# RWKV groups 1 to 3 of a hybrid decoder trunk: whole value projection ahead of the triangular matrices, output projection between and behind them

## The chip, the cores and the metric

The kernel runs on one core of one Trainium2 chip. The metric is the device time of one execution in microseconds (us), where less is better; the time of a kernel is the median of several runs. A change of 0.5% is about what a measurement of this kernel can tell from no change.

## What is computed

One RWKV-7 time-mixing layer with its SwiGLU, then one layer of dilated sliding-window attention with its SwiGLU, on 256 tokens of 1024 columns in float32. The change lies in the time mixing:

```python
def rwkv7_time_mix(x, ...):
    h = rms_norm(x, norm_g)
    dx = jnp.pad(h, ((0, 0), (1, 0), (0, 0)))[:, :-1] - h
    xr, xw, xk, xv, xa, xg = (h + dx * mu[i] for i in range(6))
    r = xr @ w_r
    ...
    k = xk @ w_k
    v = xv @ w_v
    ...
    o = wkv7_scan(rh, decay, kh, vh, -kk, kk * ah)
    ...
    o = (o - mean) * lax.rsqrt(var + LNX_EPS)
    o = o.reshape(Bn, Sn, Dn) * lnx_g.astype(f32) + lnx_b.astype(f32)
    bonus = jnp.sum(rh * kh * r_k.astype(f32), axis=-1, keepdims=True) * vh
    y = (o + bonus.reshape(Bn, Sn, Dn)) * g.astype(f32)
    return y.astype(x.dtype) @ w_o, v_first
```

The scan is computed in chunks: products of decayed keys give triangular matrices over 128 tokens, and (1 - triangle) is inverted block by block.

## The kernel before, in words

Time mixing runs in four **groups** of four heads (256 columns); `group(it)` exists once for each engine (PE L631, ACT L1170, DVE L1676), and each engine works through its own list in the order of the code, held to the others by semaphores alone. A group projects r, k and v, builds the matrices for two chunks (c = 0, 1) of 128 tokens, inverts them, applies them, and normalises the output. From group 1 on weights and inputs are split in a high and a low float32r part, and a product is three matmuls (hi by hi, lo by hi, hi by lo; `PASSES`). Group 0 uses float32 and has no work left over (`behind=False`).

The output projection of group it - 1 (`product_o(it)`, L598) runs inside group it. It multiplies the gated output y (`y_hi`, `y_lo`) by `ow_hi` and the low part of w_o: two tiles of 128 tokens by two halves of 512 columns, six matmuls of 512 columns each. The result goes to the PSUM banks of `WO_BANKS` (L243), and DVE adds it to the residual stream x (`add_output`, L1670, one call for each of four quarters; it counts `dve_xadd`).

**PE, group 1 to 3.** Second rank of the decays; r; v quarter 0 (12 matmuls of 256 columns); `turn_norms`; v quarter 1; `product_o` tile 0; wait for `dve_scaled` (all inputs of the matrices); matrices of c = 0 (eight matmuls); `product_o` tile 1; matrices of c = 1; then the inversion levels l = 1 to 5 (L751). Each level is X products for heads 0 to 3 and 4 to 7, U products for both, and a filler, `values_fill(l)` (L710): v quarter 2 between the two X products of level 1 (l = 0), v quarter 3 and transposes of the keys after level 1, then bonus and gate in levels 2 and 3, the turned values in level 4, a product with `Vn` in level 5. After the levels come transposes (L782), the last block of the inversion, `next_keys(v)`, which is a quarter of the next group's k projection (in group 3, matmuls that only keep the clock), and the state.

**DVE, group 1 to 3.** Norms of the last group's output, scans, gates; then `gate_output` (L1659: two `stt`, a sync, and y + bonus), the copy of the next gains to `pl`, `decayed_keys`, the low part of y after ACT has made `y_hi`, `receptances`, `unit_keys`, and the last product, which counts `dve_scaled`. Then `add_output` 0 and 1; the masked copies of the c = 0 matrices, a reduction and a block transpose (T, counted by `dve_T`); `add_output` 2 and 3; the same for c = 1; and the levels. `low_key_weights(0)` and `(1)` (L1706) follow levels 1 and 2: the low part of the next group's k weights, one half each.

**ACT, group 3** (L1170 on): after the matrices it waits for `pe_v`, issues the load of a norm gain, copies `vT`, copies the turned keys, and then

```python
act.wait_ge(s_gu[0], 32)
A(wsp[:, 1, 0, 0:2048], raw[0][:, 0:2048], ACT.Copy).then_inc(S("act_gu_hi"), 1)
act.wait_ge(s_dn[0], 16)
A(wsp[:, 1, 0, 2048:3072], raw[0][:, 2048:3072], ACT.Copy).then_inc(S("act_dn_hi"), 1)
...
act.wait_ge(S("pe_g"), it + 1)
...
A(gT, bank[5], ACT.Copy).then_inc(S("act_g"), 1)
act.wait_ge(S("pe_tv"), it + 1)
A(Vn.rearrange("p c n i -> p (c n i)"), bank[6], ACT.Copy).then_inc(S("act_vn"), 1)
```

The first two copies are the high parts of the first gate/up and down weights of the feed-forward part. The four copies of the inverted blocks to `Us` (L1263) follow. In groups 1 and 2 the copies of the next group's `rw_hi` and of `ow_hi` (which waits for this group's w_o weights, `s_wm[3]`, and for all four quarters of `product_o`) stand where group 3 has the feed-forward ones.

**SP** issues the loads in one list: for each group k, r, w_o (`load_out`, L392) after `pe_wo` has counted all quarters of `product_o`, v after `pe_v`, and the second-rank weights. At the end of the list for time mixing stand

```python
sp.wait_ge(S("pe_wo"), NGRP * 4 - 4)
load_out(NGRP - 1)
```

and right behind, with no wait of their own that is still open there, the feed-forward loads: gate/up (two of 512 KB) and down (512 KB) for slot 0, the same for slot 1.

Of the kernel before, what the change touches and what calls it, by code (L numbers as in the profile page):

```python
# [16 lines left out]
ALU = mybir.AluOpType  # L17
# [71 lines left out]
def program(nc, ins, out):  # L89
    ctx = ExitStack()  # L90
    with ctx:
# [150 lines left out]
        HALVES = (slice(0, KT * T // 2), slice(KT * T // 2, KT * T))  # L242
        WO_BANKS, WO_LAST = (0, 1, 7, 0), (0, 1, 5, 7)  # L243
        EARLY = 2
# [248 lines left out]
        def _(pe):  # L493
# [104 lines left out]
            def product_o(it, tiles=range(RT), done=0, halves_=range(2)):  # L598
# [8 lines left out]
                for r in tiles:  # L607
                    for j in halves_:
                        if r == 1 and j == 1 and it < NGRP:
                            pe.wait_ge(S("dve_xadd"), it * 4 - 3)  # L610
                        o = bank[(WO_BANKS if it < NGRP else WO_LAST)[2 * r + j]]
# [19 lines left out]
            def group(it, behind=True, ahead=True):  # L631


                def next_keys(v):
                    if ahead:
                        if v == 0:
                            pe.wait_ge(S("dve_x_lo"), 2)
                            pe.wait_ge(S("dve_mix_lo"), it * 6 + 2)
                        project_parts(7, 1, kw_hi, (xk_hi, xk_lo), "pe_k", [v])
                    else:  # L640
                        keep_clock((4, 4, 4, 3)[v], 7)
# [45 lines left out]
                if behind:  # L687
                    turn_norms()
                    values([early - 1])
                    pe.wait_ge(S("act_sa"), it + 1)  # L690
                    product_o(it, [0])
                pe.wait_ge(S("dve_scaled"), it + 1)
                for c in range(2):
                    if c == 1:
                        if behind:
                            product_o(it, [1])
                        else:
                            values([early - 1])
# [11 lines left out]
                def values_fill(l):  # L710

                    if l == 0:
                        values(range(early, 3))
                    elif l == 1:
                        values(range(max(early, 3), 4))
                        for j, src in enumerate((kP, bP)):
# [34 lines left out]
                for l in range(1, LEVELS - 1):  # L751
                    corner = l == LEVELS - 2
                    for q in range(2):
                        pe.wait_ge(S("dve_T"), it * 10 + 2 * l + q - 1)
                        if l == 1 and q == 0 and behind:
                            pe.wait_ge(S("dve_xadd"), it * 4)
                        for u in range(4 * q, 4 * q + 4):
# [736 lines left out]
        def _(dve):  # L1494
# [143 lines left out]
            def norm_output(it, c, meanwhile=None, squaring=None):  # L1638
# [18 lines left out]
                tt(on[:, c, :, :].rearrange("p n (h i) -> p (n h) i", h=2), occ, wide_[1], ALU.mult).then_inc(S("dve_on"), 1)  # L1657

            def gate_output(it, c=None):  # L1659

# [15 lines left out]
            def group(it, behind=True, ahead=True):  # L1676
# [97 lines left out]
                if behind:  # L1774
                    gate_output(it)
                    q.mark(dve.tensor_copy(pl[:, :, :], par[:, two, lg:lg + 2]))
                    decayed_keys()
                    dve.wait_ge(S("act_y_hi"), it)
                    low_part(y_lo[:, :, :], yT[:, :, :], y_hi[:, :, :], "dve_y_lo")
                    receptances()  # L1780
# [19 lines left out]
                if behind:  # L1800
                    add_output(it, [0, 1])
                def turn_blocks(h):
# [5 lines left out]
                for c in range(2):  # L1808
# [10 lines left out]
                    if behind and c == 0:  # L1819
                        add_output(it, [2, 3])  # L1820
                    if not behind and c == 0:
# [3 lines left out]
                for l in range(1, LEVELS - 1):  # L1825
# [9 lines left out]
                    for h in range(2):  # L1835
# [7 lines left out]
                        else:  # L1843
                            for o, i in PAIRS:
                                m = dve.tensor_copy(Us[o, us, i], new[o])
                            m.then_inc(S("dve_U"), 1)
                    if ahead and l in (1, 2):
                        low_key_weights(l - 1)
                    if l == 3:
# [5 lines left out]
                for n in range(2):  # L1855
                    cut = slice(n * T, (n + 1) * T)
                    m = stt(bv[:, cut], bv[:, cut], pl[:, n, 1:2], gT[:, cut], ALU.add, ALU.mult)
                q.mark(m)
                for h in range(2):
                    dve.wait_ge(S("pe_X"), it * 12 + 11 + h)  # L1860
# [313 lines left out]
```

## Time and profile before

| What | Value |
|---|---|
| median of 3 runs | 937.66 us (937.49 to 942.2) |
| the profiled execution: time | 938.9 us |
| its span | 936.6 us |
| granted TensorE clock, mean of the span | 0.996 |
| PE / DVE / ACT / POOL busy | 919.4 / 685.3 / 501.9 / 100.5 us |
| time mixing, groups 1 to 3 | about 88 to 266 us of the span |

All times in the rows below count from the start of the span. L495 is the line of the matmul helper `mm`, L1496 and L1499 are `tt` and `stt`, L1102 is ACT's helper: the tile names tell the operations apart. `wide` is banks 3 to 6 of PSUM, `bank` the others.

### The profile page before, as it was taken

The numbers are of one execution on the slowest core, as the hardware profiler recorded it, in microseconds if no ns is written. First come the engines' busy times: TensorE is split into PE (matmuls) and PEld (weight loads), VectorE is DVE, ScalarE is ACT, GpSimd is POOL, SyncE is SP. The second block draws the span as 40 slices with busy tenths as digits, with TensorE's granted clock in tenths as the row PEclk, the third lists the DMA queues.
The fourth block names the chain that finished last, engine by engine and source line by source line (L and its number), as shares of the span: only waits on it lengthen the run. The fifth ranks groups of instructions, "written<-read, shape, count | busy, mean of one in ns | idle before, by whom it ended". The sixth has DMA issues, their size and how long they took to land.

```text
span 936.6 us, 18302 instructions
## 1 busy us (share of the span) xinstructions
PE 919.4 (98%) x7008; PEld 814.7 (87%) x7008; DVE 685.3 (73%) x1286; ACT 501.9 (54%) x818; POOL 100.5 (11%) x75
## 2 busy tenths in 40 slices
PE   9999999999999999999999999999999999999998
PEld 7779789898879888888899999999998798888887
DVE  7877877868666766666687889888878666666665
ACT  4554544435344544444467776777677445445442
POOL 0200100001012000000041133213221000000000
PEclk9999999999999999999999999999999999999999
DMA  9311212201517676667369545544554246776661
GB/s 296 132 58 48 91 59 91 98 7 54 155 41 197 173 224 179 186 193 219 105 204 293 154 134 159 155 142 137 168 158 113 79 138 188 202 202 186 193 180 46
DMA packets 195241, 136.71 MB, mean 146 GB/s; under 512 B 7390, under 2 KB 186078, under 8 KB 195180
## 3 DMA queue, kind: packets, MB, share of 16 engines
q1 hardware_dynamic: 194748, 135.13, 49.2%
q8 instruction: 44, 0.72, 0.3%
q10 hardware_dynamic: 432, 0.72, 0.3%
q14 instruction: 17, 0.14, 0.0%
HBM read 134.78 MB, written 1.05 MB: 145 GB/s over the span
## 4 chain that ended last, share of the span: by engine, by line
PE 88%; DVE 7%; ACT 3%; issue 1%; DMA 1%; POOL 0%; SPq 0%; DVEq 0%; ACTq 0%
PE bank L495 50%; PE wide L495 34%; DVE work L1496 2%; ACT work L1102 1%; DVE work L1811 1%; DVE work L1499 1%; DVE work L1815 1%; PE wide L1045 1%; PE bank L1045 1%; ACT L1102 1%; DMA x<-in_x 1%; DVE x L1496 1%; PE wide L1022 0%; PE bank L1022 0%; ACT Vs L1102 0%
## 5 line engine op out<-in xcount | busy, mean ns | idle before, releaser
L495 PE MATMUL bank<-wpj,hkq 128*128 128x384 f32 x1152 | 215.6, 340 | 1.5 <-ACT Vs L1102 0.4
L495 PEld LDWEIGHTS bank<-wpj,hkq 128*128 128x128 f32 x1152 | 197.6, 188 | 6.2 <-issue 4.2
L495 PE MATMUL wide<-hsp,wsp 128*128 128x256 f32 (+2 forms) x1120 | 196.2, 328 | 0.0
L495 PEld LDWEIGHTS wide<-hsp,wsp 128*128 128x128 f32 x1120 | 172.4, 190 | 22.5 <-DVE hsp L1496 0.6
L1496 DVE TENSOR_TENSOR wsp<-ring,wsp 128x1024 fp32r<-128x1024 f32 (+1 forms) x88 | 150.7, 1752 | 4.3 <-ACT wsp L1102 4.2
L1102 ACT ACTIVATE wsp<-ring 128x1024 fp32r<-128x1024 f32 (+1 forms) x88 | 130.4, 1485 | 27.4 <-DMA ring<-in_f_w_gu 15.8
L2100 POOL TENSOR_TENSOR gsm<-gsm,mhalf 128x6 f32<-128x6 f32 (+1 forms) x40 | 74.3, 1877 | 315.8 <-DVE gsm L2018 174.1
L1102 ACT ACTIVATE rows<-wide 128x256 f32<-128x256 f32 x66 | 25.4, 384 | 145.8 <-PE wide L495 145.7
L495 PE MATMUL bank<-wsp,asp 128*128 128x512 f32 x396 | 98.1, 392 | 0.0
L1496 DVE TENSOR_TENSOR wpj<-ring,wpj 128x1536 fp32r<-128x1536 f32 x48 | 84.1, 1753 | 17.1 <-ACT wpj L1102 17.1
L495 PEld LDWEIGHTS bank<-wsp,asp 128*128 128x128 f32 x396 | 71.7, 189 | 13.1
L1102 ACT ACTIVATE work<-wide 128x256 f32<-128x256 f32 (+3 forms) x73 | 30.8, 441 | 91.4 <-PE wide L495 42.9
L1102 ACT ACTIVATE wpj<-ring 128x1536 fp32r<-128x1536 f32 x48 | 71.1, 1486 | 6.4 <-PE bank L495 6.3
L495 PE MATMUL bank<-work 64*64 64x32 f32 (+7 forms) x1216 | 68.4, 233 | 3.2 <-DVE work L1803 1.5
L495 PEld LDWEIGHTS bank<-work 64*64 64x64 f32 (+4 forms) x1216 | 56.2, 136 | 17.3 <-issue 5.6
L1496 DVE TENSOR_TENSOR am<-sg,rows 128x256 f32<-128x256 f32 x44 | 18.8, 426 | 71.7 <-ACT sg L1102 71.1
L495 PE MATMUL bank<-hsp,wsp 128*128 128x256 f32 (+1 forms) x368 | 68.7, 329 | 0.0
L495 PE MATMUL wide<-work 64*64 64x32 f32 (+6 forms) x720 | 62.2, 263 | 3.1 <-DVE work L1496 2.8
L495 PEld LDWEIGHTS bank<-hsp,wsp 128*128 128x128 f32 x368 | 56.9, 190 | 6.2
L495 PEld LDWEIGHTS wide<-work 64*64 64x64 f32 (+4 forms) x720 | 53.8, 158 | 7.8 <-DVE work L1496 5.2
L1496 DVE TENSOR_TENSOR rows<-wide,rows 128x256 f32<-128x256 f32 x66 | 27.9, 424 | 37.6 <-ACT rows L1102 37.6
L495 PE MATMUL wide<-wsp,asp 128*128 128x512 f32 x132 | 37.1, 389 | 0.0
(290 smaller groups left out, 1336.2 us busy)
## 6 DMA issues: line engine op xcount, KB each, us to landing
ring<-in_f_w_gu SPq DMA_DIRECT2D x88, 512.0 KB, 6.1
ring<-in_w_kv SPq DMA_DIRECT2D x96, 256.0 KB, 3.5
ring<-in_f_w_down SPq DMA_DIRECT2D x44, 512.0 KB, 3.7
ring<-in_b_w_q SPq DMA_DIRECT2D x48, 256.0 KB, 3.5
wmix<-in_a_w_k SPq DMA_DIRECT2D x4, 1024.0 KB, 5.9
wmix<-in_a_w_r SPq DMA_DIRECT2D x4, 1024.0 KB, 5.4
wmix<-in_a_w_v SPq DMA_DIRECT2D x4, 1024.0 KB, 5.2
wmix<-in_a_w_o SPq DMA_DIRECT2D x4, 1024.0 KB, 5.1
```

Source lines behind the costliest of these rows:

```text
L495: return pe.matmul(o, a, b, start=start, stop=stop)
L1045: m = pe.transpose(SCORES[r][h][:, j * P:(j + 1) * P], pr[r][:, h, j * P:(j + 1) * P], ident)
L1102: return act.activation(o, i, f, **k)
L1496: return dve.tensor_tensor(o, a, b, op)
L1499: return dve.scalar_tensor_tensor(o, a, s, b, op0, op1)
L1811: dve.copy_predicated(M[:, 4 * c + h:4 * c + 4:2, 0:2, :], tri.rearrange("p (u m) t -> p u m t", u=2), bank[MB[h]].rearrange("p (u m t) -> ...
L1815: step(dve.tensor_reduce(Tq[:, us, :], M[:, us, 0, :].rearrange("p u (b t) -> p u t b", t=QB), AX.X, ALU.add))
L2100: return pool.tensor_tensor(dst, src, mhalf[:, 0:n], ALU.pow)
```

## The change

Groups 1 to 3 (`behind=True`) alone, but for `low_key_weights`, whose calls move in groups 0 to 2. PE does all four v quarters before the matrices, `product_o` tile 0 between c = 0 and c = 1, and tile 1 as the two fillers of level 1, its last quarter into bank 5. The waits on `dve_xadd` become later or are dropped. DVE gets `gate_turned` (the two `stt` of the gating only); y + bonus, the copy to `pl` and the low part of y move behind `dve_scaled`; `add_output` 0 and 1 go to where 2 and 3 stood, 2 and 3 behind level 1; `low_key_weights(0)` goes behind level 2 and `(1)` behind the gated bonus after the levels. Nothing is changed in the lists of ACT, SP and POOL.

```diff
--- before.py
+++ after.py
@@ -240,7 +240,7 @@
         mix_lo = wmix_low[:, :, :].rearrange("p a d -> p (a d)").rearrange("p (i n) -> p i n", i=4)
         rw_hi, kw_hi, ow_hi = x_hi[:, 2, :], w_hi[:, 0, :], w_hi[:, 1, :]
         HALVES = (slice(0, KT * T // 2), slice(KT * T // 2, KT * T))
-        WO_BANKS, WO_LAST = (0, 1, 7, 0), (0, 1, 5, 7)
+        WO_BANKS, WO_LAST = (0, 1, 7, 5), (0, 1, 5, 7)
         EARLY = 2
         MB, MK = (3, 4), (2, 5)
 
@@ -606,8 +606,6 @@
                         pe.wait_ge(s_wm[3], it * 16)
                 for r in tiles:
                     for j in halves_:
-                        if r == 1 and j == 1 and it < NGRP:
-                            pe.wait_ge(S("dve_xadd"), it * 4 - 3)
                         o = bank[(WO_BANKS if it < NGRP else WO_LAST)[2 * r + j]]
                         for n in range(2):
                             cut = slice(j * 512, (j + 1) * 512)
@@ -635,7 +633,8 @@
                     if ahead:
                         if v == 0:
                             pe.wait_ge(S("dve_x_lo"), 2)
-                            pe.wait_ge(S("dve_mix_lo"), it * 6 + 2)
+                        if v < 2:
+                            pe.wait_ge(S("dve_mix_lo"), it * 6 + v + 1)
                         project_parts(7, 1, kw_hi, (xk_hi, xk_lo), "pe_k", [v])
                     else:
                         keep_clock((4, 4, 4, 3)[v], 7)
@@ -686,14 +685,13 @@
                 values(range(early - 1))
                 if behind:
                     turn_norms()
-                    values([early - 1])
+                    values(range(early - 1, 4))
                     pe.wait_ge(S("act_sa"), it + 1)
-                    product_o(it, [0])
                 pe.wait_ge(S("dve_scaled"), it + 1)
                 for c in range(2):
                     if c == 1:
                         if behind:
-                            product_o(it, [1])
+                            product_o(it, [0])
                         else:
                             values([early - 1])
                     for banks, src, read in ((MB, bP, 2), (MK, kP, 4)):
@@ -710,9 +708,15 @@
                 def values_fill(l):
 
                     if l == 0:
-                        values(range(early, 3))
+                        if behind:
+                            product_o(it, [1], halves_=[0])
+                        else:
+                            values(range(early, 3))
                     elif l == 1:
-                        values(range(max(early, 3), 4))
+                        if behind:
+                            product_o(it, [1], halves_=[1])
+                        else:
+                            values(range(max(early, 3), 4))
                         for j, src in enumerate((kP, bP)):
                             for n in range(2):
                                 m = pe.transpose(bank[4][:, (2 * j + n) * P:(2 * j + n + 1) * P], src[:, n, 0:P], ident)
@@ -753,7 +757,7 @@
                     for q in range(2):
                         pe.wait_ge(S("dve_T"), it * 10 + 2 * l + q - 1)
                         if l == 1 and q == 0 and behind:
-                            pe.wait_ge(S("dve_xadd"), it * 4)
+                            pe.wait_ge(S("dve_xadd"), it * 4 - 2)
                         for u in range(4 * q, 4 * q + 4):
                             for i, o in PAIRS if corner else zip(BLK, BLK):
                                 w = corners[q][i, u % 4, o] if corner else M[i, u, 0, o]
@@ -1656,6 +1660,14 @@
                 dve.wait_ge(S("pool_ors"), it * 2 + (c - 1))
                 tt(on[:, c, :, :].rearrange("p n (h i) -> p (n h) i", h=2), occ, wide_[1], ALU.mult).then_inc(S("dve_on"), 1)
 
+            def gate_turned(it):
+
+                dve.wait_ge(S("pe_on"), it)
+                for n in range(2):
+                    cut = slice(n * T, (n + 1) * T)
+                    m = stt(yT[:, n, :], bank[2][:, cut], pl[:, n, 0:1], gT[:, cut], ALU.mult, ALU.mult)
+                q.mark(m)
+
             def gate_output(it, c=None):
 
                 cut = slice(0, T) if c is None else slice(c * P, (c + 1) * P)
@@ -1772,11 +1784,8 @@
                     tt(v4(flat(kP)), v4(flat(kT_)), v4(En), ALU.mult)
 
                 if behind:
-                    gate_output(it)
-                    q.mark(dve.tensor_copy(pl[:, :, :], par[:, two, lg:lg + 2]))
+                    gate_turned(it)
                     decayed_keys()
-                    dve.wait_ge(S("act_y_hi"), it)
-                    low_part(y_lo[:, :, :], yT[:, :, :], y_hi[:, :, :], "dve_y_lo")
                     receptances()
                     unit_keys()
                 else:
@@ -1798,7 +1807,11 @@
                     q.mark(dve.tensor_copy(pl[:, :, :], par[:, two, lg:lg + 2]))
                     low_half("xk", 1)
                 if behind:
-                    add_output(it, [0, 1])
+                    q.sync()
+                    tt(yT.rearrange("p n t -> p (n t)"), yT.rearrange("p n t -> p (n t)"), bv, ALU.add).then_inc(S("dve_y"), 1)
+                    q.mark(dve.tensor_copy(pl[:, :, :], par[:, two, lg:lg + 2]))
+                    dve.wait_ge(S("act_y_hi"), it)
+                    low_part(y_lo[:, :, :], yT[:, :, :], y_hi[:, :, :], "dve_y_lo")
                 def turn_blocks(h):
                     dve.transpose(Tq[:, 4 * h:4 * h + 4, :].rearrange("p u t -> p (u t)"),
                                   Uc[:, 4 * h:4 * h + 4, :].rearrange("p u t -> p (u t)")).then_inc(S("dve_T"), 1)
@@ -1817,7 +1830,7 @@
                     dve.wait_ge(S("dve_U"), it * 12 + c + 1)
                     turn_blocks(c)
                     if behind and c == 0:
-                        add_output(it, [2, 3])
+                        add_output(it, [0, 1])
                     if not behind and c == 0:
                         dve.wait_ge(S("act_x_hi"), 2)
                         dve.wait_ge(S("pe_r"), 1)
@@ -1844,8 +1857,10 @@
                             for o, i in PAIRS:
                                 m = dve.tensor_copy(Us[o, us, i], new[o])
                             m.then_inc(S("dve_U"), 1)
-                    if ahead and l in (1, 2):
-                        low_key_weights(l - 1)
+                    if behind and l == 1:
+                        add_output(it, [2, 3])
+                    if ahead and l == 2:
+                        low_key_weights(0)
                     if l == 3:
                         dve.wait_ge(S("pe_bonus"), it + 1)
                         dve.wait_ge(S("act_v"), it + 1)
@@ -1856,6 +1871,8 @@
                     cut = slice(n * T, (n + 1) * T)
                     m = stt(bv[:, cut], bv[:, cut], pl[:, n, 1:2], gT[:, cut], ALU.add, ALU.mult)
                 q.mark(m)
+                if ahead:
+                    low_key_weights(1)
                 for h in range(2):
                     dve.wait_ge(S("pe_X"), it * 12 + 11 + h)
                     dve.tensor_copy(Xc[HD:P, 4 * h:4 * h + 4, :], bank[h][HD:P, 0:256].rearrange("p (u t) -> p u t", u=4)).then_inc(S("dve_X"), 1)
```

**PE, around the first matrices of group 1** (`xv_hi`, `x_lo`, `vw_hi` are operands of v; `y_hi`, `y_lo` of the output projection; `work` operands of the matrices). Before:

```order
L495 MATMUL bank<-w_hi,y_hi 128x512
L495 MATMUL bank<-wmix_low,y_hi 128x512
L495 MATMUL bank<-w_hi,y_lo 128x512
L495 MATMUL wide<-work 128x256 [waits dve_scaled]
L495 MATMUL wide<-work 128x256 x3
L495 MATMUL bank<-work 128x256
L495 MATMUL wide<-work 128x256
L495 MATMUL bank<-work 128x256
L495 MATMUL wide<-work 128x256
L495 MATMUL bank<-w_hi,y_hi 128x512 [waits dve_y_lo,dve_mix_lo]
```

With the change:

```order
L495 MATMUL wide<-xv_hi,vw_hi 128x256
L495 MATMUL wide<-x_lo,vw_hi 128x256
L495 MATMUL wide<-xv_hi,wmix_low 128x256
L495 MATMUL wide<-work 128x256 [waits dve_scaled,act_sa]
L495 MATMUL wide<-work 128x256 x3
L495 MATMUL bank<-work 128x256
L495 MATMUL wide<-work 128x256
L495 MATMUL bank<-work 128x256
L495 MATMUL wide<-work 128x256
L495 MATMUL bank<-w_hi,y_hi 128x512 [waits dve_y_lo,dve_mix_lo]
```

The matmuls of the output projection no longer stand ahead of the wait for `dve_scaled`; matmuls of v do, and tile 0 follows the eight matmuls of the matrices.

**PE, first level of group 1** (64x32 are the X products). Before:

```order
L495 MATMUL bank<-work 128x256
L495 MATMUL wide<-work 128x256
L495 MATMUL bank<-work 64x32 [waits dve_xadd,dve_T]
L495 MATMUL bank<-work 64x32 x7
L495 MATMUL wide<-xv_hi,vw_hi 128x256
L495 MATMUL wide<-x_lo,vw_hi 128x256
L495 MATMUL wide<-xv_hi,wmix_low 128x256
```

With the change:

```order
L495 MATMUL bank<-work 128x256
L495 MATMUL wide<-work 128x256
L495 MATMUL bank<-work 64x32 [waits dve_xadd,dve_T]
L495 MATMUL bank<-work 64x32 x7
L495 MATMUL bank<-w_hi,y_hi 128x512 [waits dve_y_lo,dve_mix_lo]
L495 MATMUL bank<-wmix_low,y_hi 128x512
L495 MATMUL bank<-w_hi,y_lo 128x512
```

The filler between the two X products is a quarter of the output projection, with its own wait, in the place of a quarter of v.

**DVE, the tail ahead of `dve_scaled` in group 1** (the row on `wide,pg` is the receptances; `y_lo` is the low part of y; `x` is the residual). Before:

```order
L1499 SCALAR_TENSOR_TENSOR work<-bank,pl,work 128x256
L1496 TENSOR_TENSOR work<-work 128x512 [waits dve_step]
L1776 COPY pl<-par 128x4
L1496 TENSOR_TENSOR work<-work 128x512 [waits act_E]
L1496 TENSOR_TENSOR y_lo<-work,y_hi 128x512 [waits act_y_hi]
L1499 SCALAR_TENSOR_TENSOR work<-wide,pg,work 128x256 [waits pe_r]
L1499 SCALAR_TENSOR_TENSOR work<-wide,pg,work 128x256
L1496 TENSOR_TENSOR work<-wide,work 128x4x128 [waits act_E]
L1496 TENSOR_TENSOR work<-work,wide 128x512 [waits pe_rn]
L1496 TENSOR_TENSOR work<-work 128x512 [waits dve_step]
L1499 SCALAR_TENSOR_TENSOR work<-work 128x4x128
L1496 TENSOR_TENSOR work<-work 128x512 [waits dve_step]
```

With the change:

```order
L1503 SCALAR_TENSOR_TENSOR work<-bank,pl,work 128x256
L1500 TENSOR_TENSOR work<-work 128x512 [waits act_E]
L1503 SCALAR_TENSOR_TENSOR work<-wide,pg,work 128x256 [waits pe_r]
L1503 SCALAR_TENSOR_TENSOR work<-wide,pg,work 128x256
L1500 TENSOR_TENSOR work<-wide,work 128x4x128 [waits act_E]
L1500 TENSOR_TENSOR work<-work,wide 128x512 [waits pe_rn]
L1500 TENSOR_TENSOR work<-work 128x512 [waits dve_step]
L1503 SCALAR_TENSOR_TENSOR work<-work 128x4x128
L1500 TENSOR_TENSOR work<-work 128x512 [waits dve_step] x2
L1812 COPY pl<-par 128x4
L1500 TENSOR_TENSOR y_lo<-work,y_hi 128x512 [waits act_y_hi]
L1824 COPY_PREDICATED work<-cst,wide 128x2x256 [waits pe_mats] x2
```

Three instructions moved behind the product that counts `dve_scaled`: y + bonus (it is the second of the x2 pair, the product the first), the copy to `pl` and the low part of y.

## Rows read from the trace of the kernel before

**Rows 1.** Page, part 1: busy time and share of each engine.

```profile
PE 919.4 (98%) x7008; PEld 814.7 (87%) x7008; DVE 685.3 (73%) x1286; ACT 501.9 (54%) x818; POOL 100.5 (11%) x75
```

**Rows 2.** Timeline, PE: start, length, instruction; triangular matrices begin, groups 1, 2, 3.

```profile
105.58 1.14 PE L495 MATMUL wide<-work 64*128 64x256 f32 x8 [0.81 <-DVE work L1496]
...
164.06 1.13 PE L495 MATMUL wide<-work 64*128 64x256 f32 x8 [0.80 <-DVE work L1496]
...
224.06 1.13 PE L495 MATMUL wide<-work 64*128 64x256 f32 x8 [0.79 <-DVE work L1496]
```

**Rows 3.** Timeline of PE in group 2, around the matrices.

```profile
158.90 0.28 PE L495 MATMUL wide<-x_lo,vw_hi 128*128 128x256 f32 x1
...
160.24 0.47 PE L495 MATMUL bank<-w_hi,y_hi 128*128 128x512 f32 x1
...
165.98 0.50 PE L495 MATMUL bank<-w_hi,y_hi 128*128 128x512 f32 x1
...
168.96 1.14 PE L495 MATMUL wide<-work 64*128 64x256 f32 x8
...
173.33 1.12 PE L495 MATMUL bank<-work 64*64 64x32 f32 x32 [0.18 <-DVE work L1803]
```

**Rows 4.** Timeline of DVE in group 2.

```profile
157.92 0.69 DVE L1496 TENSOR_TENSOR work<-work 128x512 f32<-128x512 f32 x1
...
159.40 0.69 DVE L1496 TENSOR_TENSOR y_lo<-work,y_hi 128x512 fp32r<-128x512 f32 x1
...
163.32 0.68 DVE L1496 TENSOR_TENSOR work<-work 128x512 f32<-128x512 f32 x1
...
165.22 1.34 DVE L1811 COPY_PREDICATED work<-cst,wide 128x512 f32<-128x512 int32 x2
...
170.12 1.33 DVE L1811 COPY_PREDICATED work<-cst,wide 128x512 f32<-128x512 int32 x2 [0.37 <-PE wide L495]
...
175.78 1.18 DVE L1496 TENSOR_TENSOR wmix_low<-wmix,w_hi 128x1024 fp32r<-128x1024 f32 x1
...
177.85 0.89 DVE L1496 TENSOR_TENSOR work<-bank,cst 128x256 f32<-128x256 f32 x2 [0.89 <-PE bank L495]
...
192.83 0.89 DVE L1861 COPY work<-bank 64x256 f32<-64x256 f32 x2 [1.99 <-PE bank L495]
```

**Rows 5.** Timeline, issue queues of SP and ACT in group 3.

```profile
229.06 0.37 SPq L393 DMA_DIRECT2D wmix<-in_a_w_o  x1
...
236.81 0.40 ACTq L1237 DMA_DIRECT2D gain<-in_f_norm_g  x1
```

**Rows 6.** Page, part 6: issues, KB each, us from issue to landing.

```profile
ring<-in_f_w_gu SPq DMA_DIRECT2D x88, 512.0 KB, 6.1
...
ring<-in_f_w_down SPq DMA_DIRECT2D x44, 512.0 KB, 3.7
...
wmix<-in_a_w_o SPq DMA_DIRECT2D x4, 1024.0 KB, 5.1
```

**Rows 7.** Timeline of ACT: two rows of group 2, three of group 3.

```profile
179.64 1.92 ACT L1102 ACTIVATE w_hi<-wmix 128x2048 fp32r<-128x2048 f32 x1
...
184.70 0.60 ACT L1102 ACTIVATE work<-wide 128x512 f32<-128x512 f32 x1 [3.14 <-PE wide L495]
...
240.62 1.06 ACT L1102 ACTIVATE wsp<-ring 128x1024 fp32r<-128x1024 f32 x1 [0.43 <-DMA ring<-in_f_w_down]
...
247.51 0.60 ACT L1102 ACTIVATE work<-wide 128x512 f32<-128x512 f32 x1 [2.22 <-PE wide L736]
248.01 1.67 ACT L1102 ACTIVATE work<-work 32x256 f32<-32x256 f32 x4
```

**Rows 8.** Timeline of PE in group 3: first transposes after the levels.

```profile
249.94 0.62 PE L782 MATMUL wide<-cst,work 64*64 64x64 f32 x8
```

**Rows 9.** DMA queues in the stretch 241 to 242 us; q10 is ACT's.

```profile
q10 hardware_dynamic: 65, 0.27, 76.3%
```

**Rows 10.** Stretch of group 2: busy time of each engine, PEclk, DMA share, GB/s.

```profile
196.00:197.00 1.00, 1.00 (x6) 1.00 (x6) 1.00 (x2) 0.97 (x2) 0.00 (x0) 0.50 0.00 0
```

## The prediction, made before the run

> **What bounds the kernel now.** I read the page's busy times first: PE is busy for 98% of the span [rows 1], so only PE's idle time and PE's own work can give anything. The granted clock comes next, then PE's timeline in groups 1 to 3. The reader is to see one gap at the same place in each group: PE stands idle for 0.81, 0.80 and 0.79 us ahead of the matrices, released by a DVE product [rows 2]. That is `dve_scaled`. The second gap of the stretch is 0.18 us in level 1, also released by DVE, by a block transpose [rows 3]. DVE's timeline then tells what makes `dve_scaled` late. The queues of SP and ACT come last, since `product_o` also opens the gate of a load.
>
> Group 2 stands for all three: its times are used, and what lies behind the gain is told on the clock of before, to be read as shifted with everything around it.
>
> **The change on PE, ahead of the matrices.** Twelve matmuls of `product_o` leave and 24 of v come. A quarter of v ran from 158.90, where its second matmul started, to 160.24 with eleven matmuls, so 0.122 us each, 1.46 for twelve [rows 3]. Two quarters more end at 160.24 + 2.92 = 163.16. Before, PE was through with tile 0 at 164.06 - 0.80 = 163.26 and waited to 164.06 [rows 2]. If the inputs are there, the matrices start at about 163.2: 0.80 to 0.95 us earlier, taken as **0.88 us for each of three groups, 2.6 us**.
>
> **Are the inputs there?** Ahead of `dve_scaled` DVE loses y + bonus, the copy to `pl` and the low part of y. From the start of y + bonus at 157.92 to the end of the low part at 159.40 + 0.69 = 160.09 are 2.17 us [rows 4]; of these only `decayed_keys` stays, some 0.6 of issue time, so the rest moves up by 1.5 us or a little more. The last product, at 163.32 with 0.68, then ends near 162.5: PE, due at 163.2, is covered by 0.7 us.
>
> **What comes behind it.** The three removed operations run there. From y + bonus to the low part took 159.40 - 157.92 = 1.48 us with ACT's copy in the middle [rows 4]; started at 162.4 the low part begins at 163.9 and ends at 164.6. PE wants it after the c = 0 matrices, which took 165.98 - 164.06 = 1.92 us, so at 165.1: covered by 0.5. The masked copies started 170.12 - 168.96 = 1.16 us after the matrices [rows 3, 4], so they could at 164.4 and do at 164.6 instead of 165.22. Tile 0 between the matrices takes what tile 1 took there (165.98 to 168.96), so c = 1 starts at 168.1, 0.88 early. DVE's way to the c = 1 copies has the same instructions as before, where it had 0.37 us of idle left [rows 4]. Here the second addition waits for the end of tile 0, at about 168.2, and ends at 168.9, against copies due at 168.1 + 1.16 = 169.2: cover 0.3, the thinnest of this part. Without it the gain shrinks one for one.
>
> **Level 1.** A quarter of `product_o` takes half of tile 0's 163.26 - 160.24, 1.51 us, against 1.46 to 1.54 for the quarter of v whose slot it gets: nothing, within 0.05. Additions 2 and 3 replace the low part of the k weights, 1.18 us at 175.78 [rows 4]. The fourth quarter ends where v's last did, the third addition is long done, and the fourth ends at about 176.8 + 0.7 = 177.5, ahead of 177.85, where DVE waited for PE anyway. Cover 0.35. The low part that moves behind the levels (1.2 us) falls into 1.99 us of idle ahead of 192.83 [rows 4]. Both cost nothing; without cover the state would be late by what sticks out.
>
> **The loads.** This is the part that goes against the change. Every quarter of `product_o` counts towards `pe_wo`, and `load_out` waits for the last. In group 3 it was issued at 229.06; `pe_v`, which the last quarter of `product_o` now takes the place of, came when ACT issued its own load, at 236.81 [rows 5]. So the w_o load is **7.75 us later** within the group. In groups 1 and 2 this hides: it lands 5.1 us after issue [rows 6], at 176.8 + 5.1 = 181.9, ACT copies it in 1.92 [rows 7] to 183.8, and its next copy, of the gate, started at 184.70 only [rows 7]. In group 3 the feed-forward loads stand behind it in SP's list. ACT's high part of the down weights waited for its transfer until 240.62 and took 1.06 us [rows 7]. With 7.75 added it starts at 248.4. Queued behind it on ACT are the gate, then `Vn`, then the four copies to `Us`: the gate at 249.4, `Vn` at 249.9 instead of 247.51, `Us` from 250.4 instead of 248.01, ending after 1.67 at 252.1 [rows 7]. PE waits for `Us` ahead of its transposes, which started at 249.94 [rows 8]. **Loss 2.2 us, once.**
>
> Bounds of it: the norm gain's load (ACT's queue, 512 KB) leaves the competition, being issued before the w_o load now. Were it sharing evenly, a sixth of the bytes would go (512 of 512 + 2560 KB; w_o, gate/up twice and down are 2560 [rows 6]); a sixth of the 11.56 us from the first issue to the landing is 1.9, and the loss 0.3. But its first packets lie in the stretch from 241 to 242 us [rows 9], after the down weights had landed, so I take nothing off. On the other side, nothing new competes, and 2.2 stays the upper end.
>
> The Trainium skill, page "DMA: Bandwidth & Descriptors", gives a fit for one transfer of about 2.0 us plus bytes by 436 GB/s (a fit for the software path). As an estimate by that page, the 2560 KB would land 8.0 us after the first issue, so at 244.8 here; ACT would be free at 245.9, the loss nothing and the sum -2.6. The trace does not agree: they took 240.62 - 229.06 = 11.56 us [rows 5, 7], with two more loads behind them in the queue. The sum goes by the trace.
>
> **Sum.** -3 x 0.88 + 2.2 = **-0.4 us**. The profiled execution took 938.9, the median is 937.66; the same difference on the median gives **937.2 us**, no change within the 0.5% (4.7 us) that a measurement of this kernel can tell.
>
> **Rivals.** *A: the loads do not bite.* The feed-forward weights land in time, because with the gain's load gone and the w_o load in a calmer stretch they need 2.5 us less, or ACT's order has slack that I miss. Against it: the wait for the down weights is already 0.43 us long in rows 7, so there is no slack in front. For it: the shared engines. Then -2.6: 935.0. It decides when the down weights land before 245.9. The page just named would have it so.
>
> *B: slower, by the clock.* PE's wait of 2.2 us in group 3 lies among small matmuls, and the granted clock falls behind it. The trace has such a fall in group 2, to 0.50, which is the 1.2 GHz level of the two, at 196 us [rows 10], behind a stretch of small matmuls; the time from matrices to matrices there is 224.06 - 164.06 = 60.00 us against 164.06 - 105.58 = 58.48 one group before [rows 2], so a fall costs 1.5. Then -0.4 + 1.5 = +1.1: 938.8. It decides when the wait exceeds the 0.8 us gaps, which left the clock up. Against it: the three gaps that go away could have caused falls too.
>
> *C: DVE's way is the new bound.* If ACT's round trip for the low part of y takes 0.3 us more than before, the second addition and the masked copies of c = 1 are late, and each further 0.1 costs 0.1 in three groups. At 1.2 us more nothing is left of the gain, and the loads remain: +2.2, 939.9. Against it: ACT has nothing else to do between 159.4 and 165.
>
> *D: the change moves less than it says*, since PE's work is the same and it is 98% busy: the gap goes, but returns in level 1 as a longer wait for DVE's transpose. That is a gain of 0.88 less the masked copies' lateness; at half the gain 938.5.
>
> **Numbers.** The forecast has a chance of 0.45, A 0.20, B 0.15, C 0.08, D 0.07; 0.05 is for what I do not see. The range reaches from A with the upper gain (3 x 0.95: 934.8) to between B and C, 939.4. Faster by over 0.5% needs more than all idle time that the change can reach (0.03). Slower by over 0.5% needs two of the costs at once, or runs like the one at 942.2 as median (0.05). Same: 0.92.
>
> **What would show it.** The gap before the matrices at 0 to 0.1 us in all three groups; the spacing of matrices 0.9 shorter where no fall of the clock lies between them; the w_o load of group 3 issued at about 234.2 (236.8 less 2.6); ACT idle before the copy of the down weights, which starts near 245.8; `Us` copied from 247.8; PE idle for some 2 us in level 5 and before the transposes of group 3, and nowhere else new. Wrong would be: no wait for the down weights (A), a PEclk of 0.5 in group 3 (B), masked copies of c = 1 with no idle before them (C).

## The result, and the profile with the change

| | before | with the change |
|---|---|---|
| median | 937.64 us | **941.81 us** |
| lowest to highest, 20 runs each | 935.97 to 942.97 | 939.88 to 943.28 |
| ratio | | 1.0031, 95% interval 1.0018 to 1.0043 |
| profiled execution: time, span, mean granted clock | 938.9, 936.6, 0.996 | 941.47, 939.2, 0.991 |

The change made the kernel slower: +4.17 us by the medians, +0.3% by the ratio, whose interval leaves 1 out. By the means of the 20 runs it is 941.54 - 938.43 = +3.1 us, because three of the runs before took 942 us or more; the size is known no better than that. The change of time is within the 0.5% called no change ahead of the run, but the time lies above the range of 934.8 to 939.4. The forecast said 0.4 us faster.

**The gap before the matrices is gone.** PE's timeline, where the matrices of c = 0 begin, has no idle in front of them any more; columns as in [rows 2]:

```profile
103.46 1.14 PE L495 MATMUL wide<-work 64*128 64x256 f32 x8
...
160.95 1.13 PE L495 MATMUL wide<-work 64*128 64x256 f32 x8
...
219.94 1.13 PE L495 MATMUL wide<-work 64*128 64x256 f32 x8
```

From group 1 to group 2 are 160.95 - 103.46 = 57.49 us, against 58.48 before; from 2 to 3 58.99 against 60.00 [rows 2], where both executions have a short fall of the clock in between, some 3.4 us long. So 0.99 and 1.01 us less. The matrices of group 1 start 2.12 us earlier, but 1.25 of that comes from ahead of 88 us, where nothing was changed: the profiled execution of before has a fall of the clock there (PEclk 0.77, 0.50, 0.50 and 0.52 from 55 to 59 us), that of the changed kernel has none. This part is left out of what follows, and 0.87 us remain for group 1. I measure from the matrices of group 3 on.

**DVE in group 2, against [rows 4].** The low part of y now stands between the product and the masked copies:

```profile
159.54 1.29 DVE L1500 TENSOR_TENSOR work<-work 128x512 f32<-128x512 f32 x2
160.75 0.17 DVE L1812 COPY pl<-par 128x4 f32<-128x4 f32 x1
161.53 0.69 DVE L1500 TENSOR_TENSOR y_lo<-work,y_hi 128x512 fp32r<-128x512 f32 x1 [0.61 <-ACT y_hi L1106]
162.14 1.33 DVE L1824 COPY_PREDICATED work<-cst,wide 128x512 f32<-128x512 int32 x2
...
165.22 1.44 DVE L1500 TENSOR_TENSOR x<-bank,x 128x512 f32<-128x512 f32 x2
167.03 1.33 DVE L1824 COPY_PREDICATED work<-cst,wide 128x512 f32<-128x512 int32 x2 [0.37 <-PE wide L495]
```

The copies start 162.14 - 160.95 = 1.19 us after the matrices, and those of c = 1 still find 0.37 us of idle ended by PE, the same as in [rows 4]. DVE's part holds PE up no more than before: in level 1 PE waits for it 0.6 us in three waits, before 0.5.

**Group 3 is where the time goes.** SP's queue issues the w_o load and the feed-forward loads behind it; ACT's timeline shows what they do there (to be read against [rows 5, 7]):

```profile
232.66 0.37 SPq L393 DMA_DIRECT2D wmix<-in_a_w_o  x1
233.08 1.09 SPq L423 DMA_DIRECT2D ring<-in_f_w_gu  x2
234.22 3.48 SPq L429 DMA_DIRECT2D ring<-in_f_w_down  x1
```

```profile
242.42 2.86 ACT L1106 ACTIVATE wsp<-ring 128x2048 fp32r<-128x2048 f32 x2 [8.66 <-DMA ring<-in_f_w_gu]
245.18 1.06 ACT L1106 ACTIVATE work<-wide 128x512 f32<-128x512 f32 x2
246.13 1.67 ACT L1106 ACTIVATE work<-work 32x256 f32<-32x256 f32 x4
```

ACT waits 8.66 us for gate/up, copies both weights, and only then the gate with `Vn` (245.18) and `Us` (246.13). PE's timeline and its waits (engine and line, releaser: us, times, longest) from 88 to 267 us:

```profile
244.38 0.44 PE L495 MATMUL wide<-work 32*32 32x32 f32 x16
246.30 1.97 PE L495 MATMUL wide<-work 128*128 128x64 f32 x8 [1.48 <-ACT work L1106]
248.20 1.06 PE L786 MATMUL wide<-cst,work 64*64 64x64 f32 x8
249.19 2.07 PE L495 MATMUL bank<-cst 128*128 128x128 f32 x8
```

```profile
PE wide L495 <- ACT work L1106: 1.5, 1, 1.5
PE bank L495 <- DVE work L1816: 0.6, 3, 0.2
```

The 2.4 us that PE waited for DVE in three gaps of 0.8 are no longer among the waits; one of 1.5 for ACT is. But the first row behind it is odd: eight matmuls in 1.97 us. The busy time by stretches says why (length, busy time of each engine with its instructions, PEclk, DMA share, GB/s):

```profile
244.00:245.00 1.00, 0.72 (x32) 0.61 (x32) 0.72 (x4) 1.00 (x2) 0.00 (x0) 1.00 1.16 293
245.00:246.00 1.00, 0.00 (x0) 0.00 (x0) 0.92 (x4) 1.00 (x3) 0.00 (x0) 0.75 1.16 352
...
246.00:259.00 13.00, 12.70 (x76) 12.07 (x77) 3.84 (x5) 4.05 (x11) 0.00 (x0) 0.50 0.19 58
...
259.00:260.00 1.00, 1.00 (x11) 1.00 (x10) 0.20 (x1) 0.00 (x0) 0.00 (x0) 0.92 1.07 311
```

The clock falls to the lower level, 1.2 GHz, inside PE's wait, and stays there for the 13 us to 259: 13.7 us with the two edges (half of 245 to 246, a sixth of 259 to 260). Before, it stood at 1.00 through all of this part:

```profile
245.00:265.00 20.00, 19.68 (x279) 18.51 (x275) 11.50 (x29) 5.62 (x15) 1.01 (x1) 1.00 0.21 57
```

**The bill of group 3**, from the first matrices to the first matmul of the last output projection. Before, 264.95 - 224.06 = 40.89 us; with the change 267.79 - 219.94 = 47.85:

```profile
267.79 3.65 PE L495 MATMUL bank<-wmix,work 128*128 128x512 f32 x8
```

That is +6.96, and with 0.87, 0.99 and 1.01 us gained in the three groups, +4.1, close to the difference of the medians. The experiments divide the 6.96 between the late loads, the wait and the clock.

### The profile page after: what moved, and what is told of

The parts are those of the page before. It is cut to its first block, busy times and chain, and to the rows that moved or that the text cites. A ratio compares the mean times of both kernels' runs of the same rounds, so it can differ in the third digit from the quotient of the medians.

```text
span 939.2 us, 18308 instructions
## 1 busy us (share of the span) xinstructions
PE 923.4 (98%) x7008; PEld 819.5 (87%) x7008; DVE 685.2 (73%) x1286; ACT 501.9 (53%) x818; POOL 100.3 (11%) x75
## 4 chain that ended last, share of the span: by engine, by line
PE 91%; DVE 5%; ACT 2%; DMA 1%; issue 1%; POOL 0%; SPq 0%; DVEq 0%; ACTq 0%
PE bank L495 50%; PE wide L495 36%; DVE work L1500 1%; DMA ring<-in_f_w_gu 1%; DVE work L1824 1%; DVE work L1828 1%; PE wide L1049 1%; PE bank L1049 1%; DVE x L1500 1%; PE wide L1026 0%; PE bank L1026 0%; ACT Vs L1106 0%; PE bank L518 0%; ACT work L1106 0%; POOL gsm L2117 0%
## 5 line engine op out<-in xcount | busy, mean ns | idle before, releaser
L495 PEld LDWEIGHTS bank<-work 64*64 64x64 f32 (+4 forms) x1216 | 58.4, 139 | 18.0 <-issue 5.8
L495 PE MATMUL bank<-work 64*64 64x32 f32 (+7 forms) x1216 | 70.6, 236 | 3.2 <-DVE work L1816 1.6
```

Source lines behind the costliest of these rows:

```text
L495: return pe.matmul(o, a, b, start=start, stop=stop)
```

## The experiments

Each kernel is compared with runs of before on the same chip in the same session; the medians of before were 937.51 us (`e1_early` to `e4_fill`), 938.35 (`e5b_before_early`, `e6b_pe_only`) and 937.45 (the last three).

**The loads out of the way.** In `e1_early` the feed-forward loads of slot 0 go ahead of the w_o load, behind none of PE's products:

```diff
-            sp.wait_ge(S("pe_wo"), NGRP * 4 - 4)
-            load_out(NGRP - 1)
...
                 for b in range(2):
+                    if layer == 0 and b == 0:
+                        sp.wait_ge(S("pe_wo"), NGRP * 4 - 4)
+                        load_out(NGRP - 1)
```

> The changed kernel, but SP issues the feed-forward loads of slot 0 (gate/up, down) right after the r projection of group 3, ahead of the wait for the output projection and of the w_o load; slot 1 follows the w_o load. Theory (the loads were late, PE waited for ACT, and the granted clock fell behind that wait): ACT has no wait for these weights, PE no idle in level 5 of group 3, no fall of the clock there; the gain ahead of the matrices (about 0.97 us in each of three groups) stands alone: 2.9 us under the kernel before, 934.7. Rival (the new order costs something elsewhere in groups 1 to 3, for example the w_o and v loads issued back to back): still 938 or more.

Measured: 934.95 us (932.24 to 937.1, 8 runs), ratio to before 0.996 [0.9944, 0.9976]. ACT's copies follow their predecessor with no wait:

```profile
231.96 2.86 ACT L1107 ACTIVATE wsp<-ring 128x2048 fp32r<-128x2048 f32 x2
```

The late loads are the cause of the loss: with them early the change is 2.6 us faster than before, as three gaps of 0.88 promise. One part of the expectation failed, the clock. In the profiled execution (937.1 us) PE waits for nobody in group 3, and the clock falls all the same:

```profile
244.00:245.00 1.00, 1.00 (x13) 0.84 (x13) 0.97 (x3) 0.80 (x3) 0.00 (x0) 1.00 0.00 0
245.00:246.00 1.00, 1.00 (x7) 1.00 (x6) 0.01 (x1) 0.19 (x1) 0.00 (x0) 0.51 0.00 0
...
254.00:255.00 1.00, 1.00 (x7) 1.00 (x7) 0.00 (x0) 0.00 (x0) 0.00 (x0) 0.50 1.13 335
255.00:256.00 1.00, 1.00 (x10) 1.00 (x9) 0.58 (x2) 0.00 (x0) 0.00 (x0) 0.87 1.15 299
```

`e2_reorder` is milder: only `load_out` moves, between the slots, and the wait for `pe_wo` stays ahead of everything.

```diff
             sp.wait_ge(S("pe_wo"), NGRP * 4 - 4)
-            load_out(NGRP - 1)
...
+                    if layer == 0 and b == 0:
+                        load_out(NGRP - 1)
```

> The changed kernel, with the same list of loads and the same wait for the output projection, but the w_o load of group 3 stands between slot 0 and slot 1 of the feed-forward loads. 1.5 MB instead of 2.5 MB have to land before ACT goes on: 0.6 of the 11.56 us, so about 7 us after 232.7, at 239.7, before ACT gets to the gate at 240. Theory (the amount in front of the down weights makes the wait): 934.7, as with the early loads. Rival (it is the late issue itself that costs, whatever stands in front): 940 or more.

Measured: 935.38 us (934.69 to 937.22, 11 runs), 0.9969 [0.9955, 0.9982]: the same as `e1_early`. Here ACT does wait. The gate comes 1.1 us later within the group than in `e1_early` (239.98 - 218.21 = 21.77 us after the matrices, against 20.62), but `Vn` does not, and PE waits for neither:

```profile
237.22 2.86 ACT L1107 ACTIVATE wsp<-ring 128x2048 fp32r<-128x2048 f32 x2 [5.17 <-DMA ring<-in_f_w_gu]
239.98 0.58 ACT L1107 ACTIVATE work<-wide 128x512 f32<-128x512 f32 x1
```

So it is enough that the 1024 KB of w_o no longer stand in front. Its profiled execution has the same fall without a wait: 263.38 - 218.21 = 45.17 us for group 3, as `e1_early` with 263.41 - 218.25 = 45.16.

**The lateness alone.** `e3_before_late` is the kernel before with one line: SP waits for the last v product ahead of group 3's w_o load. That puts the load 236.43 - 223.70 = 12.73 us behind the first matrices of the group, against 5.00 before and 12.72 with the change.

```diff
+            sp.wait_ge(S("pe_v"), NGRP)
             sp.wait_ge(S("pe_wo"), NGRP * 4 - 4)
```

> The kernel before, with nothing changed but one wait of SP: the w_o load of group 3 and the feed-forward loads behind it wait until the v projection of group 3 is done, 7.75 us later than they were. Theory (late loads, wait and clock together cost 7 us in group 3): 944.6. Only the wait of about 2.2 us and no fall of the clock: 939.8. Rival (the loss of the changed kernel comes from its new order of matmuls): 937.6.

Measured: 946.3 us (943.54 to 949.97, 6 runs), 1.0082 [1.006, 1.0105].

```profile
236.43 0.37 SPq L393 DMA_DIRECT2D wmix<-in_a_w_o  x1
...
236.44 0.41 ACTq L1238 DMA_DIRECT2D gain<-in_f_norm_g  x1
...
248.16 2.85 ACT L1103 ACTIVATE wsp<-ring 128x2048 fp32r<-128x2048 f32 x2 [10.11 <-DMA ring<-in_f_w_gu]
...
252.04 1.97 PE L496 MATMUL wide<-work 128*128 128x64 f32 x8 [3.45 <-ACT work L1103]
```

Late loads alone, with no other part of the change, cost 8.8 us by the medians. In the profiled execution, the slowest of the six (949.97 us), gate/up took 248.16 - 236.43 = 11.73 us from the w_o issue, against 242.42 - 232.66 = 9.76 with the change, so that PE's wait is 3.45 us. The sign is shown; the size of the change's cost is not to be taken from this run.

The trace tells where the 2 us arose. Here ACT issued its 512 KB for the norm gain right behind the w_o load. DMA queues of the stretches 238 to 240 and 240 to 242 us (q1 is SP's, q10 ACT's; packets, MB, share of the 16 engines):

```profile
q1 hardware_dynamic: 60, 0.25, 55.1%
q10 hardware_dynamic: 64, 0.26, 33.6%
...
q1 hardware_dynamic: 121, 0.50, 60.9%
q10 hardware_dynamic: 78, 0.26, 34.2%
```

The gain's load moved beside w_o's, and w_o landed 7.0 us after its issue, against 5.0 with the change, where the gain's load was issued at 227.40 and q10 was empty from 232 us on. So this run has a second load in the way that the change does not have. That it accounts for all of the 2 us was not tested.

**The wait with the clock kept up.** `e4_fill` is the changed kernel with eight matmuls of no use where PE waits in group 3, so that the wait stays and the idle goes (`keep_clock(n, b)` multiplies constants n times into bank b):

```diff
                     elif l == 5:
+                        if not ahead:
+                            keep_clock(5, 7)
                         pe.wait_ge(S("act_vn"), it * 2 + 1)
...
+                if not ahead:
+                    keep_clock(3, 7)
                 pe.wait_ge(S("act_g"), it + 1)
```

> The changed kernel with its late loads, but PE runs eight matmuls of 128 by 128 that nobody reads in the wait of group 3: five ahead of the wait for Vn in level 5 and three ahead of the wait for the copies to Us, about 0.27 us each. They change nothing in what ACT waits for. Theory (the clock falls because PE has nothing to do, and that is two thirds of the loss): the clock stays up, the wait of about 2.2 us remains: 937.64 - 2.9 + 2.3 = 937.0. Rival (the wait itself, or the small matmuls around it, cost the 7 us): 941.8 as the changed kernel.

Measured: 936.65 us (935.57 to 938.97, 12 runs), 0.9987 [0.9973, 1.0].

```profile
244.66 1.10 PE L495 MATMUL wide<-work 128*128 128x64 f32 x8 [0.30 <-ACT work L1110]
...
246.42 0.63 PE L790 MATMUL wide<-cst,work 64*64 64x64 f32 x8
...
261.44 3.65 PE L495 MATMUL bank<-wmix,work 128*128 128x512 f32 x8
```

```profile
244.00:259.00 15.00, 14.55 (x141) 13.61 (x139) 6.68 (x14) 5.37 (x15) 1.01 (x1) 1.00 0.33 98
```

The clock is at 1.00 throughout, and the same eight matmuls on 64 columns take 1.10 us where they took 1.97. Group 3 takes 261.44 - 218.17 = 43.27 us. This divides the bill: **43.27 - 40.89 = 2.4 us are the wait, 47.85 - 43.27 = 4.6 us the clock.** A second cut through the same rows agrees. The transposes behind the levels start 248.20 - 219.94 = 28.26 us after the matrices with the change and 246.42 - 218.17 = 28.25 here, against 249.94 - 224.06 = 25.88 before [rows 2, 8]. So the wait is the same 2.4 us in both, and the 4.6 us lie wholly behind it: from there on the changed kernel takes 47.85 - 28.26 = 19.6 us and this one 43.27 - 28.25 = 15.0. The 2.4 us of the wait are more than the 1.48 us of idle in front of the product with `Vn`, since the transposes need `Us` as well, whose copies ACT ended at 247.8. 5.2 us of the median came back with eight matmuls added.

**Do early loads help by themselves?** `e5b_before_early` is the kernel before with the edit of `e1_early` and nothing else.

> The kernel before with the early loads of e1_early and nothing else. ACT's wait for the down weights was 0.4 us there and PE never waited for it, so theory: no change, 937.5 within 0.5. Rival (the early loads are a gain of their own, so that e1_early's gain is not the order's): 935 or 936.

Measured: 937.35 us (936.69 to 942.92, 12 runs), 0.9992 [0.9974, 1.001]. Nothing gained: the three gaps stand at 0.80 us, and group 3 takes 262.07 - 221.19 = 40.88. So the 2.6 us of `e1_early` are the moved products, not the loads.

**PE's part without DVE's.** `e6b_pe_only` is `e1_early` with DVE's tail as before: y + bonus, the copy and the low part ahead of `dve_scaled` again.

```diff
-                    gate_turned(it)
+                    gate_output(it)
+                    q.mark(dve.tensor_copy(pl[:, :, :], par[:, two, lg:lg + 2]))
                     decayed_keys()
+                    dve.wait_ge(S("act_y_hi"), it)
+                    low_part(y_lo[:, :, :], yT[:, :, :], y_hi[:, :, :], "dve_y_lo")
...
```

> The changed kernel with early loads, but DVE's tail ahead of the matrices as before the change: y + bonus, the copy to pl and the low part of y stand ahead of the last product again. PE's order and the places of the additions to x are those of the change. Theory (DVE's 1.6 us shorter way is what lets PE go on; PE's order alone swaps one filler of 2.9 us for another): the gap of 0.8 us ahead of the matrices is back in each group, 937.5. Rival (PE's order gives a part of it): 935 to 936.5.

Measured: 937.82 us (935.67 to 940.1, 12 runs), 0.9993 [0.9978, 1.0008]. The gap is back, three times 1.0 us at most, in PE's waits:

```profile
PE wide L496 <- DVE work L1501: 2.9, 3, 1.0
```

Without the three instructions' move on DVE, then, the new order on PE gains nothing. DVE's move with PE's old order was not run: there `product_o` tile 0 stands ahead of the matrices and waits for the low part of y.

**Can the fall without a wait be kept off?** `e7b_early_fill3` is `e1_early` with `keep_clock(3, 7)` in level 5 of group 3; `e8b_early_fill8` has the eight matmuls of `e4_fill`; `e9b_early_again` is `e1_early` once more for comparison.

> e1_early with three matmuls of 128 by 128 that nobody reads, ahead of the product with Vn in level 5 of group 3, where PE has no wait to hide them: 0.8 us of work added. e1_early's profile has a fall of the clock right behind level 5, though PE waits for nothing there; it cost 45.16 - 40.88 = 4.3 us from the matrices of group 3 to the first float32 matmul on w_o, and six of its eight runs took 934.6 or more against 932.3 of the other two. Theory (level 5 and what follows leave PE too little to do, and three denser matmuls hold the clock): all runs at 932.3 + 0.8 = 933.1. Rival (they do not hold it): 935.8, e1_early and the added work.

> e1_early with the eight filling matmuls of e4_fill. If e4_fill's fillers were covered by the wait, they cost their 2.2 us here: 932.3 + 2.2 = 934.5, the clock up in group 3. If they were not covered there, the two kernels with fillers differ by more than the remaining 0.3 us of wait: below 934.

> e1_early once more, beside the two kernels with fillers, for its share of runs without a fall of the clock: median 935, lowest 932.3, as before; the profile shows whether group 3 takes 40.9 us (clock up) or 45.2 us (clock down) from its matrices to the first float32 matmul on w_o.

Measured: 934.34 us (932.8 to 936.9), 937.99 (934.29 to 939.41) and 934.57 (932.12 to 938.53), 12 runs each; ratios 0.9965 [0.9951, 0.9978], 0.9988 [0.997, 1.0006] and 0.9969 [0.9954, 0.9983]. Three matmuls change nothing that can be measured against `e9b_early_again`: six runs of `e7b_early_fill3` are at a mean clock of 1.0 against two, too few to tell, and neither its theory (all runs at 933.1) nor its rival (935.8) came true. Eight cost 3.4 us, which I had not expected. Sorting the runs by their mean granted clock explains a part of it. Medians of the runs with one clock, in us, with their number; the few runs at 0.994, 0.995, 0.997 and 0.999 are left out:

| mean clock | before, 3 sessions | `e1_early` and again | `e7b` | `e8b` | `e4_fill` | the change |
|---|---|---|---|---|---|---|
| 1.0 | none | 932.3 (2), 932.9 (2) | 933.3 (6) | none | 936.0 (4) | none |
| 0.998 | 937.2 (46) | 934.6 (2), 934.4 (6) | 934.9 (3) | 936.2 (4) | 936.8 (5) | none |
| 0.996 | 938.4 (18) | 935.7 (3), 935.5 (1) | 936.1 (3) | 938.2 (4) | 938.6 (2) | none |
| 0.989 to 0.993 | 942 to 942.7 (9) | none | none | none | none | 940 to 942.8 (20) |

At 0.998 `e8b` is 1.8 us above `e9b`, which is what its group 3 shows too (262.16 - 219.44 = 42.72 against 40.85 in `e9b`); the rest is that more of its runs lie at 0.996 or less, 7 of 12 against 3, for which I have no cause. `e4_fill` is 2.2 to 2.4 us above `e1_early` at 0.998, the wait once more. And all 20 runs of the change lie at 0.993 or less, which is about (1 - 0.993) x 2 x 938 = 13 us or more at the lower level, as long as this one fall. `e1_early`, its repetition and `e2_reorder` have 5 of 31 runs at 0.994 and none below, and of the 12 runs of `e4_fill` one is at 0.994 and none below. Where in the kernel the clock was low is known for the profiled executions alone; that it was group 3 in each of the 20 runs is read from these means, not seen.

## Why the prediction was wrong

**Where the gap goes: right, a little small.** Predicted 0.88 us in each group; measured 0.99 and 1.01 with a short fall between, and 0.95 between groups without one (`e4_fill`, 160.64 - 103.11 = 57.53, against 58.48). The thinnest cover held: 0.37 us before the copies of c = 1 (predicted 0.3), and PE has no wait for the additions. C and D fell with it.

**The loads: the mechanism right, the exact agreement partly luck.** The issue was to come 7.75 us later within the group and came 12.72 - 5.00 = 7.72 later. The down copy was to start 240.62 + 7.75 - 224.06 = 24.31 us after the matrices; it started at 244.2, 24.3 after them. But it did not start there for the reason given. Down landed at 234.2 + 9.5 = 243.7, 11.1 us after the first issue instead of 11.56. What held ACT was gate/up, which landed 9.76 us after the first issue where it had taken at most 238.28 - 229.06 = 9.2 before, and whose own copy of 1.9 us now came behind the wait instead of ahead of it. The two errors cancel. PE's loss from the wait was predicted at 2.2 and measured at 2.4. Rival A fell. To take nothing off for the gain's load did no harm to the sum.

The estimate by the Trainium skill (page "DMA: Bandwidth & Descriptors", section "Anatomy of one DMA — SWDGE (gpsimd) path"), by which there would be no loss, fails here: the page's fit for the 2048 KB of w_o and gate/up gives 6.8 us, an estimate. The trace has 9.76.

**The step that failed is the clock: the sum has no term for it.** The sum puts -2.6 for the gaps and +2.2 for the wait and takes the clock in group 3 as unchanged; the fall stands there as rival B alone, with 0.15 and a price of 1.5. Measured, it is a term of +4.6 us. "So a fall costs 1.5" was taken from the fall of group 2. The stretches around [rows 10] show how short that one was:

```profile
195.00:196.00 1.00, 1.00 (x9) 1.00 (x9) 1.00 (x1) 0.34 (x1) 0.00 (x0) 0.74 0.00 0
...
198.00:199.00 1.00, 1.00 (x7) 1.00 (x6) 0.39 (x1) 0.00 (x0) 0.00 (x0) 0.55 0.00 0
```

It lasted 0.5 + 2 + 0.9 = 3.4 us. The one in group 3 lasted 13.7 us and cost 4.6; that of `e1_early` lasted 10.2 us (1.0 of the stretch from 245, 9 from 246 to 255, 0.3 of the last) and cost 45.16 - 40.85 = 4.3. So a fall had no fixed price here: it took 1.5 of 3.4, 4.3 of 10.2 and 4.6 of 13.7 us. PE ran matmuls of 256 columns during the fall of group 2, twelve of them for the next group's k; in group 3, where there is no next group, it ran matmuls of 64 and 128 columns. Whether that difference set how long the falls lasted was not tested, so the length of group 3's fall stays open. I gave B 0.15, with the argument that gaps of 0.8 us left the clock up. Here the wait was 1.5 us, behind a stretch of small matmuls; the clock fell inside it in the profiled run, and the mean clocks point to as long a stretch in all 20.

With the numbers put right, the sum is -3 x 0.95 + 2.4 + 4.6 = +4.15 us, against +4.17 by the medians and +3.1 by the means. So close an agreement is luck: the terms come from one profiled execution of each kernel.

**What stays open:** why the clock fell in the profiled executions of `e1_early` and `e2_reorder`, at 245 us, with PE never idle there, and why nine of the 76 runs of before lie at 0.992 or less. So PE's idle is not the only thing that a fall at this place can come from. What is shown is that keeping PE busy through this wait kept it up in the profiled run and brought the median down by 5.2 us.

**What beats both kernels:** `e1_early`, 934.95 and 934.57 us in two sessions, 2.6 and 2.9 us under the kernel before (0.3 to 0.4%, both intervals below 1, but less than the 0.5% called no change), 7 under the change as made. It keeps the moved products and moves two lines of SP's list.

## What to carry to other kernels

When work moves behind another product, look at every counter which that product feeds, and on through the load it opens to the last queue behind it: here 1 MB for a later use stood ahead of 1.5 MB for an earlier one, and only the order of two issues decided between +4 and -3 us. Give the clock a term in the sum when PE gets a new wait: list what PE has behind the wait, and look up in a trace what such work takes at the lower clock (here the eight matmuls of 64 columns took 1.97 us instead of 1.10). A price taken from another fall holds for a fall of that length only, so note how long that one lasted.

## What the hardware did that I had not expected

- In the profiled execution the clock fell inside a wait of 1.48 us and was back 13.7 us later, with PE busy for 12.7 of the 13 us from 246. The fall of group 2 ended after 3.4 us.
- Matmuls of 128x128 in place of the idle kept it at 1.00, and the eight 128x64 matmuls behind them ran in 1.10 us instead of 1.97.
- Two executions fell to 0.50 with no idle on PE before (`e1_early`, `e2_reorder`), for a cost of 4.3 us each.
- The same three loads in the same order took 9.76 us to the landing of gate/up in one kernel and 11.73 us in another, where a 512 KB load of ACT's queue moved beside them.
